# First two modulation vectors by column units, with six weight tiles multiplied between the loads

## The reference, cut to what matters

```python
c_act = silu(c)
mod = c_act @ w_ada + b_ada                    # [2048] @ [2048, 6*2048]
sh1, sc1, gt1, sh2, sc2, gt2 = split(mod, 6)
h = rmsnorm(x, norm1_g) * (1 + sc1) + sh1      # [256, 2048]
p = h @ w_in                                   # r, k, v, low-rank inputs, pooled part
# low-rank inputs -> tanh / sigmoid -> decay, a, gate; then a recurrence over time
```

## Time and profile before

| | |
|---|---|
| median of 3 runs | 2822.28 us (2815.01 to 2830.18) |
| profiled execution | 2819.87 us, span 2818.1 us |
| mean granted TensorE clock | 0.979 |
| TensorE busy, share of the span | 96% |
| VectorE, ScalarE busy | 65%, 45% |
| granted clock in the first two of 40 slices | 0.7 |
| transfer rate in the first slice, mean over the span | 401, 197 GB/s |

### The profile page before, as it was taken

The page is one execution under the profiler, slowest core; times in us unless marked ns, Lnnn a source line. Parts: engine busy times, 40 slices in busy tenths (PEclk is TensorE's granted clock), DMA queues, the critical chain, the costliest instruction groups (busy, mean ns, idle before and its releaser), DMA issues.

```text
span 2818.1 us, 47810 instructions
## 1 busy us (share of the span) xinstructions
PE 2697.9 (96%) x17516; PEld 2224.6 (79%) x17516; DVE 1825.9 (65%) x2529; ACT 1260.3 (45%) x1712; POOL 143.7 (5%) x149
## 2 busy tenths in 40 slices
PE   5799999989999999999999999999999999999998
PEld 0357667777888888888888888887878888888887
DVE  0455565666877777755576676678577777776554
ACT  1432222244555555544443355643455555554443
POOL 1001100321000000010100000000100000000000
PEclk7799999999999999999999999999999999999999
DMA  9776655434555555555555544444545555555553
GB/s 401 286 293 252 236 229 227 173 115 162 187 193 188 184 193 192 185 205 208 196 185 180 192 163 153 162 164 166 192 161 182 189 183 187 185 183 205 206 197 134
DMA packets 82701, 554.73 MB, mean 197 GB/s; under 512 B 8496, under 2 KB 8624, under 8 KB 17840
## 3 DMA queue, kind: packets, MB, share of 16 engines
q1 hardware_dynamic: 81888, 550.21, 53.1%
q10 hardware_dynamic: 720, 3.21, 0.3%
HBM read 551.29 MB, written 2.10 MB: 196 GB/s over the span
## 4 chain that ended last, share of the span: by engine, by line
PE 86%; DVE 6%; DMA 3%; ACT 2%; issue 2%; DVEq 0%; SPq 0%; ACTq 0%
PE bank L516 52%; PE bank L517 26%; DMA raw<-in_stream_dram 3%; PE bank L559 2%; DVE wlo L1460 1%; PE bank L683 1%; DVE yb L1476 1%; PE bank L697 1%; PE bank L693 1%; DVE zmat L1695 0%; DVE t L1583 0%; DVE yb L2065 0%; PE bank L775 0%; PE bank L781 0%; PE bank L768 0%
## 5 line engine op out<-in xcount | busy, mean ns | idle before, releaser
L516 PE MATMUL bank<-act,whi 128*128 128x512 f32 x4976 | 1785.2, 403 | 24.4 <-DVE act L1497 20.9
L517 PE MATMUL bank<-act,wlo 128*128 128x256 f32 x4976 | 1396.5, 281 | 0.0
L516 PEld LDWEIGHTS bank<-act,whi 128*128 128x128 f32 x4976 | 940.7, 189 | 279.3 <-issue 38.6
L1460 DVE TENSOR_TENSOR wlo<-raw,whi 128x1024 fp32r<-128x1024 f32 x846 | 1035.2, 1232 | 177.8 <-ACT whi L1034 171.5
L1034 ACT ACTIVATE whi<-raw 128x1024 fp32r<-128x1024 f32 x846 | 883.5, 1052 | 438.4 <-PE bank L517 409.0
L517 PEld LDWEIGHTS bank<-act,wlo 128*128 128x128 f32 x4976 | 944.8, 190 | 3.6 <-issue 3.4
L516 PE MATMUL bank<-ff,whi 128*128 128x512 f32 x1408 | 493.2, 393 | 1.0 <-DVE wlo L1460 1.0
L517 PE MATMUL bank<-ff,wlo 128*128 128x256 f32 x1408 | 392.8, 279 | 0.0
L516 PEld LDWEIGHTS bank<-ff,whi 128*128 128x128 f32 x1408 | 263.8, 187 | 64.6 <-DVE wlo L1460 1.6
L517 PEld LDWEIGHTS bank<-ff,wlo 128*128 128x128 f32 x1408 | 263.8, 187 | 0.0
L1476 DVE TENSOR_REDUCE joined<-bank 128x256 f32<-128x512 f32 x179 | 123.4, 691 | 212.2 <-PE bank L517 212.0
(11 more groups left out here) (236 smaller groups left out, 1518.4 us busy)
## 6 DMA issues: line engine op xcount, KB each, us to landing
raw<-in_stream_dram SPq DMA_DIRECT2D x519, 1024.0 KB, 4.8
x<-in_x_dram SPq DMA_DIRECT2D x1, 2048.0 KB, 14.4
lora_w<-in_lora_dram SPq DMA_DIRECT2D x1, 1536.0 KB, 11.6
pool_w<-in_pool_w_dram ACTq DMA_DIRECT2D x1, 1024.0 KB, 8.8
out_dram<-x SPq DMA_DIRECT2D x2, 512.0 KB, 2.8
out_dram<-x ACTq DMA_DIRECT2D x2, 512.0 KB, 3.0
catt<-in_att_dram ACTq DMA_DIRECT2D x1, 576.0 KB, 3.4
par<-in_params_dram SPq DMA_DIRECT2D x1, 541.5 KB, 3.3
```

The source lines that it names most:

```text
L516: nc.tensor.matmul(tile_bank(t), wh, flat(pair[:, kt]), start=starts and n == 0, stop=False)
L517: mm = nc.tensor.matmul(small_half(t), wl, pair[:, kt, 0], start=False, stop=stops and last)
L1460: nc.vector.tensor_tensor(wlo[:, k % RING], raw[:, r % RING, 8 * (k % 2):8 * (k % 2) + 8], whi[:, k % RING].bitcast(F32), ALU.subtract).th ...
```

## The change

The first two vectors are made in eight units of 256 columns. Unit u loads four parts: for each of the two vectors two times eight row tiles, 256 columns wide, so that a load is 1 MiB in lines of 1 KB. After the four parts comes one load of 0.75 MiB: of six weight tiles (three low-rank ones and the first three of `wkv`) the row tiles 2u and 2u+1, also in 1 KB lines. After the parts of a unit `ada_row` is copied, and four products with `pick` give the columns of shift and scale for two row tiles; these two tiles of activations are filled, and two units later (`six_rows`, after part 1) the twelve pairs with the six weight tiles are multiplied. The six tiles gather in six banks; their joins and the low-rank functions come in a new `opening`. That has ten steps in place of sixteen, with one chunk of the third vector in steps 0 to 3 and two in steps 4 to 9; its `preparation` parts are placed by `OPEN_PREPARATION`. x is loaded ahead of all chunks. The statistics of x are taken in unit 1. In the new order the places 40 and on are: weight 8, weight 9, chunk 0, weight 10, chunks 1 and 2, weight 11, chunks 3 to 5, weight 12 (place 50), chunks 6 to 9 (51 to 54), weight 13 (55), chunks 10 to 15 (56 to 61). VectorE cuts the second half of weight 12 in step 7, that of weight 13 in step 9.

```diff
-LORA_AT = {0: (0, 1), 2: (2,), 4: (3,)}
+LORA_AT = {1: (0, 1), 2: (2,), 3: (3,)}
+OPEN_PREPARATION = {3: (1, 4), 6: (7,), 7: (8,), 8: (9, 10), 9: (14,)}
...
-    w = FIRST_CHUNK["wkv"]
-    order = [("w", c) for c in range(w + 2)]
-    c, a = w + 2, 0
-    for s in range(NGROUP):
+    order = []
+    for u in range(UNITS):
+        order += [("first", 4 * u + q) for q in range(4)] + [("w", u)]
+    order += [("w", UNITS), ("w", UNITS + 1)]
+    c, a = UNITS + 2, 0
+    for m in range(OPEN_STEPS):
+        if m in (1, 3, 5, 7):
+            order.append(("w", c))
+            c += 1
+        for _ in range(1 if m < 4 else 2):
+            order.append(("ada", a))
+            a += 1
+    for s in range(1, NGROUP):
...
-            for r in range(2):
-                load((r, 0, 0))
             sp.dma_start(x[:], x_in).then_inc(x_loaded, 16)
-            for r in range(2, RING):
-                load((r, 0, 0))
-
-
-            with sp.Fori(1, ADA0 // RING) as i:
-                for q in range(RING):
-                    sp.wait_ge(ada_used, RING * i + (q - 3))
-                    load((q, i, RING))
+
+            def load_unit(r):
+
+                u, part = divmod(ORDER[r][1], 4)
+                first = KT * (part // 2) + 8 * (part % 2)
+                src = stream[first:first + 8, :, 2 * P * u:2 * P * u + 2 * P].rearrange("k p n -> p k n")
+                dst = raw[:, r % RING].rearrange("p (k two) n -> p k (two n)", two=2)
+                sp.dma_start(dst, src).then_inc(raw_full[r % RING], 16)
...
+            def load_six(r):
+
+                u = ORDER[r][1]
+                src = stream[RAW[0]:RAW[0] + FIRST_SIX, :, 2 * P * u:2 * P * u + 2 * P].rearrange("j p n -> p j n")
+                dst = raw[:, r % RING, 0:2 * FIRST_SIX].rearrange("p (j two) n -> p j (two n)", two=2)
+                sp.dma_start(dst, src).then_inc(raw_full[r % RING], 16)
...
+            for r in range(5 * UNITS):
+                if r >= RING:
+                    freed(r - RING)
+                if ORDER[r][0] == "first":
+                    load_unit(r)
+                else:
+                    load_six(r)
+
             assert PLACE[FIRST_CHUNK["wout"]] >= LAST_ADA + RING
-            for r in range(ADA0, PLACE[FIRST_CHUNK["wout"]]):
+            for r in range(5 * UNITS, PLACE[FIRST_CHUNK["wout"]]):
                 freed(r - RING)
                 load((r, 0, 0))
-                if r == ADA0 + RING - 1:
+                if r == 5 * UNITS + 1:
...
+            def unit_part(u, part):
+
+                r = 5 * u + part
+                pe.wait_ge(raw_full[r % RING], 16 * (r // RING + 1))
+                if part == 0 and u:
+
+                    pe.wait_ge(ada_copied, u)
+                v, half = part // 2, part % 2
+                src = raw[:, r % RING].rearrange("p (k two) n -> p k (two n)", two=2)
+                for k in range(8):
+                    g = k % 4
+                    mm = nc.tensor.matmul(ada[32 * g:32 * g + 32, 2 * P * v:2 * P * v + 2 * P], crep[:, 8 * half + k], src[:, k],
+                                          start=half == 0 and k < 4, stop=half == 1 and k >= 4, tile_position=(0, 32 * g))
+                mm.then_inc(ada_used, 1)
+
+            def unit_columns(u):
+
+                pe.wait_ge(ada_copied, u + 1)
+                if u:
+                    pe.wait_ge(columns, u)
                 else:
-
-                    pe.wait_ge(mod_ready, 1)
-                    ada_turn(1)
-
-            pe.wait_ge(mod_ready, 2)
-            stat("x0")
-
-            for n in range(2 * LORA_CHUNKS):
-                full_half("lora", n, 0, 0, "h1")
+                    pe.wait_ge(picked, 1)
+                for b in range(4):
+                    mm = nc.tensor.matmul(aux[:, b:b + 1], ada_row[:, b * P:(b + 1) * P], pick[:], start=True, stop=True)
+                mm.then_inc(ada_turned, 1)
+
+            def six_rows(u):
+
+                for half in range(2):
+                    k = 2 * u + half
+                    pe.wait_ge(lo_ready, k + 1)
+                    for kt in (2 * u, 2 * u + 1):
+                        if half == 0:
+                            pe.wait_ge(a_ready, kt + 1)
+                        for j in range(3):
+                            mm = blocks_product(k, ("lora", 3 * half + j), [(2 * j + kt % 2, kt)], act2, kt == 0, kt == KT - 1)
+                    mm.then_inc(half_used, 1)
+
+            for u in range(UNITS):
+                for part in range(4):
+                    unit_part(u, part)
+                    if part == 1 and u == 1:
+                        stat("x0")
+                    if part == 1 and u >= 2:
+                        six_rows(u - 2)
+                unit_columns(u)
+            six_rows(UNITS - 2)
+            six_rows(UNITS - 1)
...
-                    for j in LORA_AT.get(n, ()):
+                placed = 0
+                for m in range(OPEN_STEPS):
+                    if m == 0:
+
+                        pe.wait_ge(tile_sum, 1)
+                    full_half("wkv", OPEN_DONE + m, 0, 0, free=m == 0)
+                    for j in LORA_AT.get(m, ()):
                         if j == 0:
 
                             pe.wait_ge(lora_loaded, 16)
                             pe.wait_ge(lora_act, 3)
+                            pe.wait_ge(tile_sum, FIRST_SIX)
                         lora_decay(j)
-                    if 5 <= n <= 8:
-                        lora_gate(n - 5)
-                    ada_chunk(ADA_PLACE[n], ADA0 + n)
-                    if n == 6:
+                    if 4 <= m <= 7:
+                        lora_gate(m - 4)
+                    for _ in range(1 if m < 4 else 2):
+                        ada_chunk(ADA_PLACE[placed], ADA0 + placed)
+                        placed += 1
+                    if m == 5:
                         kk_step(0)
-                    if n == 14:
+                    if m == 9:
...
+            for u in range(UNITS):
+                copy_unit(u)
+                if u == 0:
+                    cut_hi(0)
+                    cut_hi(1)
+                    std("x0")
+                unit_high(u)
+                if u:
+                    cut_hi(2 * u)
+                    cut_hi(2 * u + 1)
...
+            def unit_columns(u):
+
+                dve.wait_ge(ada_turned, u + 1)
+                shifts_scales = mod[:, 0:2, 2 * u:2 * u + 2]
+                bias = pcol("b_ada", 0, 2 * KT).rearrange("p (v k) -> p v k", v=2)[:, :, 2 * u:2 * u + 2]
+                nc.vector.tensor_tensor(shifts_scales, aux[:, 0:4].rearrange("p (v k) -> p v k", v=2), bias, ALU.add)\
+                    .then_inc(columns, 1)
+                dve.wait_ge(columns, u + 1)
+                if u == UNITS - 1:
+                    dve.sem_inc(mod_ready, 2 + UNIT_OFFSET)
+                pair = slice(2 * u, 2 * u + 2)
+                link(nc.vector.scalar_tensor_tensor(out=gs[:, 0, pair], in0=mod[:, 1, pair], scalar=1.0,
+                                                    in1=pcol("norm1_g", 2 * u, 2), op0=ALU.add, op1=ALU.mult))
+
+            def unit_normed(u):
+                for kt in (2 * u, 2 * u + 1):
+                    if kt >= 4:
+
+                        dve.wait_ge(a_ready, kt - 3)
+                    nc.vector.scalar_tensor_tensor(out=yb[:, kt % 4], in0=x[:, kt], scalar=gs[:, 0, kt:kt + 1], in1=rstd[:],
+                                                   op0=ALU.mult, op1=ALU.mult).then_inc(normed, 1)
+
+            def unit_low(u):
+                for kt in (2 * u, 2 * u + 1):
+                    dve.wait_ge(normed, kt + 1)
+                    dve.wait_ge(ahi_ready, kt + 1)
+                    nc.vector.scalar_tensor_tensor(out=alo[:, kt], in0=yb[:, kt % 4], scalar=mod[:, 0, kt:kt + 1],
+                                                   in1=ahi[:, kt].bitcast(F32), op0=ALU.add, op1=ALU.subtract).then_inc(a_ready, 1)
+
+            for u in range(UNITS):
+                unit_columns(u)
+                if u == 0:
+                    cut_lo(0)
+                    cut_lo(1)
+                    reciprocal_std("x0")
+                unit_normed(u)
+                unit_low(u)
+                if u:
+                    cut_lo(2 * u)
+                    cut_lo(2 * u + 1)
...
+            def opening():
+                first = 2 * FIRST_CHUNK["wkv"] + OPEN_DONE
+                cut_lo(first)
+                cut_lo(first + 1)
+                join_six(0)
+                join_six(1)
+                lora_shifted(0)
+                join_six(2)
+                lora_shifted(1)
+                join_six(3)
+                lora_shifted(2)
+                cut_lo(first + 2)
+                join_six(4)
+                shifted_tile(0, 0)
+                join_six(5)
+                shifted_tile(0, 1)
+                shifted_tile(0, 2)
+                for m in range(OPEN_STEPS):
+                    if m:
+                        cut_lo(first + 2 + m)
+                    if m % 2 == 1:
```

(64 more changed lines are left out.)

151 lines of the change are left out of this document (81 added, 70 removed).

## The result

The changed kernel takes 2838.9 us (median of 18 runs, 2825.4 to 2851.0), the kernel before 2818.2 (18 runs beside it, 2805.8 to 2830.2): ratio 1.0076, 95% interval 1.0056 to 1.0096. It is slower by 0.8%, some 21 us. The profiled execution took 2842.3 us, span 2840.5, which is 22.4 more than the one before.

What follows compares the result with a forecast made beforehand. Bound by DMA up to 91.5 us, by TensorE from 128.3 to 213.8. Six tiles done at 140, then work 63.1, waits 23.1, clock 3: end 229.3, +15.5 us, so 2838 us; range 2812 to 2864.

Steps and rivals of the forecast that it cites:

- Price of a 1 KB line: Load stage: a 1 KB line costs 46 ns, 355 GB/s, so the last part lands 30.5 us later, at 122.0.
- (b): Rival, load stage: short lines cost less; 42 ns gives +6 us, no fixed cost -2; chance 0.12.
- Ring of the load stage, tail: Load stage: ring waits add 4 us, last part at 126; a tail of 14 us ends the six tiles at 140.
- the slot of the six tiles: Load stage: ring slot held longest, 5.1 us at full clock and 11.8 at half, against about 6.5 allowed.
- Conversion under the six rows: Load stage's tail: the first six rows hide in the 6.3 us conversion; 11.5 us at full clock.
- Waits in the opening: Opening: TensorE waits for modulation chunks 1.8, 2.3, 1.5, 10.6 and 6.9 us, sum 23.1.
- Clock after the waits: Opening: a lower clock after the two waits of 7 and 11 us costs 3 us.
- Where it ended: End of the opening, where segment 1 starts: 229.3 us in place of 213.8, +15.5 us.
- (a): Rival, opening: the ring does not stall it, so it ends at 203.1, 11 us faster; chance 0.13.
- (c): Rival, load stage: short lines cost more; 65 ns gives +56 us in all, 84 ns +98; chance 0.08.
- (d): Rival, load stage: TensorE stays at 1.2 GHz there, +38 us; chance 0.07.

Runs made afterwards that it cites:

- e4_before_1k: The kernel before with its 32 first loads in lines of 1 KB, 1 MiB apart in the source, nothing else changed; ratio to the kernel before 1.0069.
- e1_order: The changed kernel with weight chunks 10 to 13 one to three places later in the opening's order of loads; 2810.1 us, ratio to the kernel before 0.9975.
- e5_cut_early: The changed kernel with VectorE's second low parts of weight chunks 11, 12 and 13 made one step earlier; 2821.3 us, ratio to the kernel before 1.0016.
- e2_lines8k: The changed kernel with the host's first 38 MiB laid out so every load of the load stage is contiguous; 2832.5 us, ratio to the kernel before 1.0045.

## Why the prediction was right

The forecast was 2838 and +15.5 us; measured 2838.9 and +20.7 of medians, +22.4 of profiles. The median of the kernel before over more runs is 4 us lower than that of the three shown, so the absolute number is nearer than the shift deserves. The mechanism was right, short loads and then a ring that stalls the opening; two of its sizes, the price of a line and the end of the six tiles, were met partly by luck. By its own steps:

- **Price of a 1 KB line.** Fitted 46 ns, 355 GB/s; measured 47 ns, 348, and the same in e4_before_1k. The number was met by luck. The 84 ns of a 2 KB line came from the share of the engines' time, because the earlier trace rows is not a full stretch. A window inside that load is full, and there the kernel before shows (534.5 to 536.5 us):

```profile
DMA packets 397, 0.81 MB, mean 407 GB/s; under 512 B 0, under 2 KB 0, under 8 KB 397
...
q1 hardware_dynamic: 397, 0.81, 104.6%
```

By the rate a 2 KB line costs 80.5 ns, not 84, and 407 GB/s stands where the prediction read 390. A straight line through the rates at 8 KB and 2 KB gives 42 ns for 1 KB, 387 GB/s, which is the case that rival (b) priced at +6. By the share of time, as the prediction read both its rows, the measured 1 KB line is 1.102 x 16 x 5 us / 1701 = 52 ns, not 46. Either way the 1 KB line costs 5 to 6 ns more than the straight line says; a share at one size and a rate at the other made the two meet. An estimate from the Trainium skill ("DMA: Bandwidth & Descriptors", Bandwidth) was about 415 GB/s at 2 KB and 398 at 1 KB: the trace nearly agrees with the first (407) and not with the second (348), so the larger cost that the prediction saw at 2 KB was not there. Why a 1 KB line costs more is open. Its distance of 1 MiB to the next is not excluded, though the 2 KB lines of the earlier trace rows lie 1 MiB apart too and reach 407. The rule of the Trainium skill on row pitches ("DMA: Bandwidth & Descriptors", Latency and other measured facts) has no measured case at 1 MiB.
- **Ring of the load stage, tail.** The last part was put at 126, so its product at 127, and all six tiles at 140; measured were 132.7 and 142.7. The loads make 2.3 us of these 5.7 (39.1 MB at 348 GB/s are 112.2 us, not 109.9); the other 3.4 go to ring and clock beyond the 4 us forecast, and 2.7 of them can be seen as the low clock of the last unit (the changed kernel beside e1_order). The tail was 3.0 us shorter than taken and hid half of that. The two sizes for the slot of the six tiles, 5.1 and 11.8 us, do not match: the second leaves out the product of part 3, and is 12.8 with it.
- **Conversion under the six rows.** It hides, as forecast: 10.0 us from the last part's product to the end of the six tiles. That is the bound at the full clock (11.5 less 1.0), not the 13 that was taken.
- **Waits in the opening.** Forecast 1.8, 2.3, 1.5, 10.6 and 6.9, sum 23.1; measured 2.38, 2.09, 1.41, 10.38 and 6.91, sum 23.2. The first fell on chunk 2, one step earlier than forecast; the other four on the chunks named (6, 7, 9, 13), and the reason holds: e1_order and e5_cut_early remove most of them from either end. These waits weigh most in the loss, and this step was right.
- **Clock after the waits.** Forecast 3 us. What the opening took beyond work and waits is 93.0 - 63.1 - 23.2 = 6.7. This term was mis-sized: four of the five waits are followed by a chunk product of 1.85 to 1.94 us, not two, and the granted clock of the opening is 0.83. In e5_cut_early TensorE does the same work of the opening in 61.4 us at a granted clock of 1.00 (141.9 to 212.1 us), so the low clock costs rather 8.4 of the 69.8 us for which it is busy here.
- **Where it ended.** Segment 1 was put at 229; the opening ended at 235.7, 2.7 us from the load stage and 3.7 from the clock.
- **Rivals.** (a) falls by the waits. (b) and (c) fall by the rate, (b) although the rows spoke for its 42 ns; the +98 for a line of 84 ns should be +102 by its own terms. (d) falls by the clock of 0.83. Short loads and waits together make the loss: the kernel is slower by 0.8% with both, by 0.5% with the waits and long loads (e2_lines8k), and faster by 0.25% with short loads and few waits (e1_order).

## What to carry to other kernels

When work is moved under a load stage, the order of everything that shares its ring has to be made anew: for each slot, name the instruction that frees it and its place in its engine's program, and compare it with the place where the load four slots on is used. A line size that no row shows is priced from rates in full stretches, all read in the same way, and even then it was 5 ns off one step beyond the rows; a layout on the host that keeps lines long gave 10.9 us of the load stage here. And when a moved block has two consumers, look for the second ring: putting the six rows last cost 6.7 to 12.6 us of the load stage, by the waits through the converted weights, which no transfer shows.

## What the runs showed of the hardware that was not expected

The packets of a queue add up to more than the engines' whole time, and the more so the shorter the line: 101% with 8 KB lines at 423 GB/s, 105% with 2 KB lines at 407, 110% with 1 KB lines at 348 (the changed kernel; 349 in e4_before_1k). The share of DMA is then no measure of the rate, and a price taken from it is too high for short lines. And the part of the kernel behind the edits, the same code each time, took from 2592 to 2614 us at a granted clock of 0.99 throughout; the cause was not looked for.
